# Split latent scores, projection pieces in the window attention, a first unit spread over the input's chunks, and earlier weight halves

## The chip, the core and the metric

The program runs on one core of a Trainium2 chip. Its engines are PE (TensorE, matrix products; PEld is its weight load), DVE (VectorE), ACT (ScalarE), POOL (GpSimd) and SP (SyncE, which here only issues DMAs). The metric is the time of one execution on the device in microseconds (us). All tensors are float32 in HBM.

## The reference

Two blocks run one after the other on a sequence of 512 tokens of width 1024, the first with 16 meta tokens ahead of it (528 in all).

```python
# first block
h = h + 0.5 * swiglu(rmsnorm(h, ffn1_norm), w1, w3, w2)          # d_ff 2816
q, k, v, u, g_attn, g_ssm = split(rmsnorm(h, mix_norm) @ w_in)
attn = sliding_window_attention(q, k, v, sinks)                  # 16 heads of 64, 4 key heads, blocks of 128
y = gelu(s5_ssm(u, ...))
ssm = (y @ ssm_glu_a) * sigmoid(y @ ssm_glu_b)
h = h + (sigmoid(g_attn) * attn + sigmoid(g_ssm) * ssm) @ w_out
h = h + 0.5 * swiglu(rmsnorm(h, ffn2_norm), w1, w3, w2)
x = rmsnorm(h, final_norm)[:, 16:]
# second block, layer 0: latent attention, 16 heads (128 without and 64 with rotation); layer 1: gated linear attention
c_q, c_kv, k_r = split(x @ w_in)                                 # 512, 256, 64
q = rms_norm(c_q) @ w_uq; k_nope = rms_norm(c_kv) @ w_uk; v = rms_norm(c_kv) @ w_uv
s = (q_nope . k_nope + rope(q_rope) . rope(k_r)) * scale         # per block of 128 queries, keys up to its end
m = softmax(mask(s)) @ v @ w_o
x = layer_norm(ALPHA * x + m); x = layer_norm(ALPHA * x + conv_ffn(x)); x = x + sigmoid(x @ w_gate + b) * (p @ w_proj)
```

## The kernel before

Activations lie transposed in SBUF, the width in 8 chunks of 128 partitions and the tokens along the free axis. A float32 product with weights is made as three `float32r` products: `mm3` (L565 to L568) multiplies high by high, high by low and low by high halves, with a weight load each. ACT writes the high half of a weight unit (128 output columns, 8 chunks) from the raw DMA buffer (`ahead_hi`, L539), DVE the low half (`ahead_lo`, L554); `feed_hi`/`feed_lo` mark the use of a unit and prepare so many units ahead. SP loads raw weights into three buffers; a buffer is reloaded when its last low half is made. A unit is 24 matmuls of 512 columns, or 48 of 264 columns in two halves of the tokens. Each engine runs its own list in the order in which the code is written; every wait is by a semaphore. `Banks` hands out the 8 PSUM banks in turn (`bk.take`) and makes PE wait until the engine that read a bank has freed it.

The stages that the change touches:

- **Setup** (`setup_*`). SP loads x in two halves of the width, 4 DMAs each, then two weights. ACT's queue loads all the small vectors of tile 0 (`vrows`, 9 DMAs). PE turns the vectors (L888), the meta tokens (L902) and x (L908, 32 transposes). Per chunk DVE copies to H (L933), ACT makes the gained high half (L813) and the square (L772), DVE the low half (L820), and POOL adds up the squares (L782). The first unit, "f1" 0, then runs in `ffn_pe` as `lin`: all 8 chunks of the tokens' first half, then all of the second.
- **State space scan** (`ssm_*`), 8 steps hq; weights of the window attention's first projections (`HEAD`: q0, q1, ga0, ga1) are fed at its end. After it ACT and DVE wait in `ssm_over` for the last y DMA, copy K, and feed the rest of `HEAD`.
- **Window attention** (`window_*`): 16 pairs (head group, block), pipelined over 20 steps i. In step i PE does values(i-4) (L1850, L1854), a whole projection unit in the steps of `WITH_UNIT` and at 17, the turns of the probabilities (i-3) (L1816, L1821), and scores(i) (L1756). DVE does softmax(i-1) (L1769, L1773), normalise(i-2) (L1795 to L1803), values (L1866), a weight's low half, its copies of the turned probabilities (L1839), the scaled projection (L836), and steps of the gelu of y. ACT does the exponentials (L1786), the high half and its copies of the turned probabilities (L1837).
- **Latent attention** (`latent_*`): 8 pairs of heads, 18 steps i, a pair's projections in every even step. In an even step PE makes qn0, qn1, qr, kn0, kn1 (`queries_pe`), the output of head i-3 (L2395), the values' projection, the turn of head i-2 (L2367), and the scores of head i (L2319, L2320), for which queries and keys stand in plain float32: 4 sets with 128, 256, 384 and 512 columns, two matmuls each. ACT copies QN and KN out of PSUM (L2282, L2286); DVE rotates the queries in `rope_dve` (4 copies of 32 partitions, L2174, and three operations, L2176 to L2180).
- **`lin_start`**, at the start of three units together (both up-projections of the convolution layers, and the `pg` gates): chunk k of units 0 and 1, and chunk k-1 of unit 2, behind each other.

## Time and profile before

| | us |
|---|---|
| median of 3 runs | 2745.61 |
| lowest and highest | 2744.53, 2750.54 |
| the profiled execution | 2743.8 |
| its span on the core | 2742.0 |
| PE busy in the span | 2676.6 |
| DVE busy | 1674.5 |
| ACT busy | 1015.2 |

The span is what the engines' records cover; 1.8 us lie around it. A busy time is the union of an engine's records. On PE a record lasts longer than the distance to the next one, since matmuls are pipelined, so the price of a matmul is read from the distance of two starts. The granted clock (PEclk) is the part of full speed that PE was given; it is 1.2 or 2.4 GHz at any moment, so a mean between 0.5 and 1 tells how much of a stretch was at 1.2.

### The profile page before, as it was taken

To read this page: it belongs to the slowest core of one execution; us is meant where nothing else is said; L and a number is where in the kernel's file an instruction comes from. 1 tells how busy PE (TensorE), PEld (TensorE's weight loads), DVE (VectorE), ACT (ScalarE), POOL (GpSimd) and SP (SyncE) were. 2 spreads that over 40 slices of the span, in tenths; PEclk is the share of its full clock that TensorE was granted. 3 is DMA by queue.
4 is the path that set the end of the run, shared out by engine and by line. 5 is a ranking of instruction groups with operands and counts; after the bars stand their busy time and mean duration, and the time that the engine had idled before them with its cause. 6 is when DMAs were issued, how large, how long until landed. Compare 5 with 4: busy or idle time off the path is not lost.

```text
span 2742.0 us, 35232 instructions
## 1 busy us (share of the span) xinstructions
PE 2676.6 (98%) x14595; PEld 2244.8 (82%) x14595; DVE 1674.5 (61%) x2553; ACT 1015.2 (37%) x1625; POOL 348.2 (13%) x361
## 2 busy tenths in 40 slices
PE   6999999988899999999999999999999999999999
PEld 6999999866687888887667688888887878888887
DVE  6754755668556544546664667737764467764765
ACT  3321333134334222333442435424454244542435
POOL 1133423020001000011000040000221014000031
PEclk9999999999899999999999999999999999999999
DMA  5243344421132233322111132332322212232231
GB/s 144 77 123 108 104 137 126 167 74 33 33 108 96 92 100 108 89 77 66 43 65 47 58 100 78 90 103 77 114 95 85 85 46 70 85 108 92 90 103 62
DMA packets 292727, 244.02 MB, mean 89 GB/s; under 512 B 19837, under 2 KB 285575, under 8 KB 292567
## 3 DMA queue, kind: packets, MB, share of 16 engines
q1 hardware_dynamic: 282503, 226.40, 26.1%
q0 software_dynamic: 5616, 13.22, 1.6%
q8 instruction: 115, 1.88, 0.3%
q10 hardware_dynamic: 4448, 2.16, 0.3%
q14 instruction: 45, 0.37, 0.0%
HBM read 230.70 MB, written 13.14 MB: 89 GB/s over the span
## 4 chain that ended last, share of the span: by engine, by line
PE 87%; DVE 8%; ACT 2%; issue 1%; DMA 1%; POOL 1%; ACTq 0%; SPq 0%; POOLq 0%; DVEq 0%
PE ps L566 26%; PE ps L567 25%; PE ps L568 25%; PE ps L2320 2%; PE ps L2319 2%; DVE ul L554 2%; PE ps L751 1%; PE ps L2395 1%; DVE rbuf L766 1%; PE ps L2367 1%; ACT S L1786 1%; ACT uh L539 1%; PE ps L3116 1%; PE ps L3092 1%; DVE tmp L2174 1%
## 5 line engine op out<-in xcount | busy, mean ns | idle before, releaser
L554 DVE TENSOR_TENSOR ul<-raw,uh 128x1024 fp32r<-128x1024 f32 (+3 forms) x416 | 526.5, 1289 | 340.5 <-ACT uh L539 340.1
L566 PE MATMUL ps<-OH,uh 128*128 128x512 f32 (+1 forms) x1736 | 646.6, 372 | 3.6 <-DVE ul L554 2.4
L568 PE MATMUL ps<-OH,ul 128*128 128x512 f32 (+1 forms) x1736 | 638.7, 368 | 0.0
L567 PE MATMUL ps<-OL,uh 128*128 128x512 f32 (+1 forms) x1736 | 638.5, 368 | 0.0
L539 ACT CAST uh<-raw 128x1024 fp32r<-128x1024 f32 (+3 forms) x416 | 411.9, 1025 | 158.3 <-PE ps L568 128.6
L566 PEld LDWEIGHTS ps<-OH,uh 128*128 128x128 f32 x1736 | 327.3, 189 | 66.6 <-issue 7.3
L567 PEld LDWEIGHTS ps<-OL,uh 128*128 128x128 f32 x1736 | 327.4, 189 | 55.2 <-issue 2.4
L568 PEld LDWEIGHTS ps<-OH,ul 128*128 128x128 f32 x1736 | 327.3, 189 | 54.6
L566 PE MATMUL ps<-XH,uh 128*128 128x264 f32 (+1 forms) x992 | 314.1, 317 | 13.4 <-DVE ul L554 8.1
L567 PE MATMUL ps<-HL,uh 128*128 128x512 f32 (+2 forms) x946 | 320.3, 339 | 0.0
L566 PE MATMUL ps<-HH,uh 128*128 128x512 f32 (+2 forms) x946 | 320.1, 338 | 0.0
L568 PE MATMUL ps<-HH,ul 128*128 128x512 f32 (+2 forms) x946 | 318.9, 337 | 0.0
L567 PE MATMUL ps<-XL,uh 128*128 128x264 f32 (+1 forms) x992 | 309.5, 312 | 0.0
L568 PE MATMUL ps<-XH,ul 128*128 128x264 f32 (+1 forms) x992 | 308.6, 311 | 0.0
L566 PEld LDWEIGHTS ps<-XH,uh 128*128 128x128 f32 x992 | 191.5, 193 | 31.1 <-DVE ul L554 8.8
L568 PEld LDWEIGHTS ps<-XH,ul 128*128 128x128 f32 x992 | 191.7, 193 | 9.1
L567 PEld LDWEIGHTS ps<-XL,uh 128*128 128x128 f32 x992 | 191.5, 193 | 8.5
L566 PEld LDWEIGHTS ps<-HH,uh 128*128 128x128 f32 x946 | 177.8, 188 | 22.8 <-issue 0.9
L567 PEld LDWEIGHTS ps<-HL,uh 128*128 128x128 f32 x946 | 177.7, 188 | 20.8 <-issue 0.5
L568 PEld LDWEIGHTS ps<-HH,ul 128*128 128x128 f32 x946 | 177.9, 188 | 19.7
L782 POOL TENSOR_TENSOR acc<-acc,tmp 128x512 f32<-128x512 f32 (+2 forms) x56 | 70.3, 1255 | 697.6 <-ACT tmp L772 693.1
L2552 POOL TENSOR_TENSOR acc<-H 128x512 f32<-128x512 f32 x4 | 8.6, 2149 | 974.3 <-DVE H L2791 623.2
(434 smaller groups left out, 3710.8 us busy)
## 6 DMA issues: line engine op xcount, KB each, us to landing
raw<-in_ffn_w SPq DMA_DIRECT2D x40, 1024.0 KB, 5.0
raw<-in_ffn_w_up SPq DMA_DIRECT2D x40, 1024.0 KB, 5.0
raw<-in_ffn_w SPq DMA_DIRECT2D x32, 704.0 KB, 4.3
raw<-in_ffn_w_down SPq DMA_DIRECT2D x32, 704.0 KB, 4.3
raw<-in_w_in SPq DMA_DIRECT2D x16, 1024.0 KB, 5.4
raw<-in_gla_w_in SPq DMA_DIRECT2D x12, 1024.0 KB, 5.0
raw<-in_mla_w_o SPq DMA_DIRECT2D x8, 1024.0 KB, 4.8
raw<-in_ple_w_gate SPq DMA_DIRECT2D x8, 1024.0 KB, 4.9
```

Of the source, the lines that this page charges most:

```text
L539: e.copy(h, src).then_inc(*s_whi.up((u, j)))
L554: e.tensor_tensor(l, src, h.bitcast(F32), SUB).then_inc(*s_wlo.up(("unit", u)))
L566: e.matmul(o, wh, xh, start=first, stop=False)
L567: e.matmul(o, wh, xl, start=False, stop=False)
L568: return e.matmul(o, wl, xh, start=False, stop=last)
L751: i = e.matmul(psum[:, b, 0:n], ones[:, :], tile[:, t0:t0 + n], start=j == 0, stop=j == len(parts) - 1)
L766: e.reciprocal(r[:, t0:t0 + n], r[:, t0:t0 + n]).then_inc(*s_dv.up((tag, "r", hf)))
L782: e.tensor_tensor(a, a, tmps[k - 1][:, t0:t0 + n], ADD).then_inc(*s_pool.up(*((tag, "acc", k, hf) for hf in hfs)))
L1786: e.activation(S_[:, r, 0:ntot], S_[:, r, 0:ntot], ACT.Exp, bias=z[:, 1, r:r + 1], accum_out=z[:, 3, r:r + 1]).then_inc(*s_fn.up())
L2174: e.tensor_copy(s[32 * k:32 * k + 32, :], P(key, 512, slice(32 * (k ^ 1), 32 * (k ^ 1) + 32))).then_inc(*s_dv.up())
L2319: e.matmul(psum[:, b, 0:N], QN[:, hh, 128 * n:128 * n + 128], KN[:, hh, 0:N], start=True, stop=False)
L2320: e.matmul(psum[:, b, 0:N], QR[p0:p0 + 64, 128 * n:128 * n + 128], KR[p0:p0 + 64, 0:N], start=False, stop=True).then_inc(*s_mm.up(("ms", h ...
```

## The change

Six things change together.

1. **Setup.** Only the vector `ffn1_norm` is loaded and turned ahead of x (`g1row`, `g1`); the rest of tile 0 is turned after the first sums of squares. The first weight's DMA is issued between the halves of x. PE turns x chunk by chunk; the last four chunks' turns alternate with the first unit's chunks, each for both halves of the tokens. Only unit 0's halves are made inside the chunk loop, unit 1's behind it. A dummy activation stands ahead of the loop on ACT.
2. **Scan's end.** Three weight units ahead are fed there in place of one.
3. **Window attention.** The 13 units (12 and the first "gs") run in pieces of chunks, `CHUNKS[i]` in step i: the rest of a begun unit behind values(i-4), a new unit's first chunks behind scores(i). They hold bank 3; the others take banks 0 to 2. DVE and ACT swap the order of some operations in a step.
4. **Latent scores.** Queries and keys are split into `float32r` halves: QNH, QNL, KNH, KNL; the rotated query's halves lie in the two halves of the partitions of one tile QA, the rotated key's halves in KRH and KRL (both hold the key twice). A set has five matmuls and at least 256 columns. The four copies of the rotation move from DVE to ACT.
5. **Latent weights.** The units uk, uv and the next uq are fed behind the copies of the step (`ahead_*`).
6. **`lin_start`.** Unit 2 runs two chunks behind.

```diff
@@ setup_sp, setup_act, setup_pe, setup_dve
-                    e.dma_start(xin[:, i, cs], x[i * 128:(i + 1) * 128, cs]).then_inc(*d_x[i].up(half))
+                    e.dma_start(xin[:, i, cs], x[i * 128:(i + 1) * 128, cs]).then_inc(*d_x[half].up("x"))
                 if half == 0:
                     e.dma_start(xme[:, :], A["meta_tokens"]).then_inc(*d_xme.up("x"))
+                    loads(e, 1)
...
+            d_g1.wait_ge(e, "row")
+            e.transpose(psum[:, b, 0:8], g1row[:, :], ident[0:8, 0:8]).then_inc(*s_mm.up("g1"))
+            for c in range(2):
+                turn_input_pe(e, c)
...
+            for c in range(2, 4):
+                turn_input_pe(e, c)
+            u = next_unit(e, "f1")
...
+            for k in range(8):
+                if k < 4:
+                    turn_input_pe(e, 4 + k)
+                s_lo.wait_ge(e, ("ffn1", k))
+                for (t0, n), key in zip(H1, keys):
+                    i = mm3(e, psum[:, bk.of[key], 0:n], hi[:, k, :], lo[:, k, :], XH[:, k, t0:t0 + n],
+                            XL[:, k, t0:t0 + n], k == 0, k == 7)
...
+            e.activation(misc[:, 3:4], one, ACT.Identity, scale=one).then_inc(*s_fn.up())
             for c in range(8):
                 if c == 4:
-                    feed_hi(e, "f1")
+                    feed_hi(e, "f1", 0)
...
+            ahead_hi(e, 1)
@@ lin_start
-            for k in range(9):
+            for k in range(10):
...
-                    if 0 <= k - j // 2 < 8:
-                        chunk(u, key, 0, k - j // 2)
+                    late = 2 * (j // 2)
+                    if 0 <= k - late < 8:
+                        chunk(u, key, 0, k - late)
@@ ssm_act, hq == 7, and ssm_dve, hq == 6
-                    feed_hi(e, HEAD[0][0])
+                    feed_hi(e, HEAD[0][0], 3)
...
-                    feed_lo(e, HEAD[0][0])
+                    feed_lo(e, HEAD[0][0], 3)
@@ window_pe
-        WITH_UNIT = (0, 1, 3, 4, 5, 6, 8, 9, 10, 11, 13, 15)
+        ALONG = [("q" if n < 2 else "ga", 2 * g + n % 2) for g in range(1, 4) for n in range(4)] + [("gs", 0)]
+        CHUNKS = (8, 8, 8, 7, 7, 7, 6, 6, 6, 6, 6, 6, 5, 5, 5, 3, 2, 2, 1, 0)
...
-            bk.limit(4)
+            bk.limit(3)
             for i in range(20):
                 if i >= 4:
                     values_pe(e, i - 4)
-                if q_ga(i):
-                    name, c = q_ga(i)
-                    lin(e, name, MIX, HR, (name, c))
-                if i == 17:
-                    lin(e, "gs", MIX, HR, ("gs", 0))
+                along_pe(e, i, True)
                 if 3 <= i <= 18:
                     turn_pe(e, i - 3)
                 if i < 16:
                     scores_pe(e, i)
+                along_pe(e, i, False)
@@ rope, queries, scores
+            for k in range(4):
+                e.copy(rope_tile(key)[32 * k:32 * k + 32, :], P(key, 512, slice(32 * (k ^ 1), 32 * (k ^ 1) + 32))).then_inc(
+                    *s_cp.up(("rope",) + key))
...
-            for k in range(4):
-                e.tensor_copy(s[32 * k:32 * k + 32, :], P(key, 512, slice(32 * (k ^ 1), 32 * (k ^ 1) + 32))).then_inc(
-                    *s_dv.up())
...
-                e.copy(QN[:, hh, :], P(("qn", p, hh, 0))).then_inc(*bk.free(s_cp, ("qn", p, hh, 0), ("qn", p, hh)))
+                e.copy(QNH[:, hh, :], P(("qn", p, hh, 0))).then_inc(*s_hi.up(("qn", p, hh)))
...
+        def queries_turned_act(e, p):
+            s_dv.wait_ge(e, ("rope", "qr", p, 0))
+            for hh in range(2):
+                rows = slice(64 * hh, 64 * hh + 64)
+                e.copy(QA[rows, hh, :], QR[rows, :]).then_inc(*s_hi.up(("qr", p, hh)))
+            feed_hi(e, "uk", 0)
...
+                e.tensor_tensor(QNL[hh][:, :], P(("qn", p, hh, 0)), QNH[:, hh, :].bitcast(F32), SUB).then_inc(
...
+                e.tensor_tensor(KNL[:, hh, :], P(("kn", p, hh, 0)), KNH[:, hh, :].bitcast(F32), SUB).then_inc(
...
+                e.tensor_tensor(QA[other, hh, :], QR[rows, :], QA[rows, hh, :].bitcast(F32), SUB).then_inc(
...
-                N = 128 * (n + 1)
+                N = max(128 * (n + 1), 256)
                 b = bk.take(e, ("ms", h, n), 4 + n)
-                e.matmul(psum[:, b, 0:N], QN[:, hh, 128 * n:128 * n + 128], KN[:, hh, 0:N], start=True, stop=False)
-                e.matmul(psum[:, b, 0:N], QR[p0:p0 + 64, 128 * n:128 * n + 128], KR[p0:p0 + 64, 0:N], start=False,
-                         stop=True).then_inc(*s_mm.up(("ms", h, n), ("ms", h)))
+                o, q = psum[:, b, 0:N], slice(128 * n, 128 * n + 128)
+                mm3(e, o, QNH[:, hh, q], QNL[hh][:, q], KNH[:, hh, 0:N], KNL[:, hh, 0:N], True, False)
+                e.matmul(o, QA[:, hh, q], KRH[:, 0:N], start=False, stop=False)
+                e.matmul(o, QA[:, hh, q], KRL[:, 0:N], start=False, stop=True).then_inc(
+                    *s_mm.up(("ms", h, n), ("ms", h)))
```

PE's list at the start of the program, before: `ident` is the identity, `xin` the input as loaded, `uh`/`ul` the weight's halves.

```order
L888 MATMUL ps<-ident,vrows 128x112
L902 MATMUL ps<-ident,xme 128x16 x8
L908 MATMUL ps<-ident,xin 128x128 x32
L566 MATMUL ps<-XH,uh 128x264
L567 MATMUL ps<-XL,uh 128x264
L568 MATMUL ps<-XH,ul 128x264
```

After:

```order
L934 MATMUL ps<-ident,g1row 128x8
L925 MATMUL ps<-ident,xin 128x128 x8
L940 MATMUL ps<-ident,xme 128x16 x8
L925 MATMUL ps<-ident,xin 128x128 x12
L572 MATMUL ps<-XH,uh 128x264
L573 MATMUL ps<-XL,uh 128x264
L574 MATMUL ps<-XH,ul 128x264
L572 MATMUL ps<-XH,uh 128x264
L573 MATMUL ps<-XL,uh 128x264
L574 MATMUL ps<-XH,ul 128x264
L925 MATMUL ps<-ident,xin 128x128 x4
```

The first unit's chunks now stand between the turns of x; chunk 0 has both halves of the tokens (two triples) before the next turn.

PE's list in the window attention from the last scores of step 7 (K and KS are keys, Q queries, PT turned probabilities, VB and V values), before:

```order
L1756 MATMUL ps<-KS,Q 128x256
L1756 MATMUL ps<-K,Q 128x16
L1756 MATMUL ps<-K,Q 128x256
L1850 MATMUL ps<-PT,VB 128x256
L1854 MATMUL ps<-PT,V 64x256 x2
L566 MATMUL ps<-XH,uh 128x512
L567 MATMUL ps<-XL,uh 128x512
```

After:

```order
L1830 MATMUL ps<-K,Q 128x16
L1830 MATMUL ps<-K,Q 128x256
L572 MATMUL ps<-XH,uh 128x512
L573 MATMUL ps<-XL,uh 128x512
L574 MATMUL ps<-XH,ul 128x512
L1924 MATMUL ps<-PT,VB 128x256
L1928 MATMUL ps<-PT,V 64x256 x2
L572 MATMUL ps<-XH,uh 128x512
```

Between the scores and the next values stood nothing; now a chunk of a projection unit does (seven, six, five and three of them in steps 3 to 6).

PE's list in the latent attention, one head's scores, before:

```order
L2319 MATMUL ps<-KN,QN 128x128
L2320 MATMUL ps<-KR,QR 128x128
L2319 MATMUL ps<-KN,QN 128x256
L2320 MATMUL ps<-KR,QR 128x256
L2319 MATMUL ps<-KN,QN 128x384
L2320 MATMUL ps<-KR,QR 128x384
L2319 MATMUL ps<-KN,QN 128x512
L2320 MATMUL ps<-KR,QR 128x512
```

After, its second and third set:

```order
L572 MATMUL ps<-KNH,QNH 128x256
L573 MATMUL ps<-KNL,QNH 128x256
L574 MATMUL ps<-KNH,QNL_158 128x256
L2432 MATMUL ps<-KRH,QA 128x256
L2433 MATMUL ps<-KRL,QA 128x256
L572 MATMUL ps<-KNH,QNH 128x384
L573 MATMUL ps<-KNL,QNH 128x384
L574 MATMUL ps<-KNH,QNL_158 128x384
L2432 MATMUL ps<-KRH,QA 128x384
L2433 MATMUL ps<-KRL,QA 128x384
```

A set of two float32 matmuls has become one of five `float32r` matmuls; the first set of the head, 128 columns before, has 256 now.

## Rows read from the trace of the kernel before

**Rows 1.** The page: busy us, share of the span and instructions by engine.

```profile
PE 2676.6 (98%) x14595; PEld 2244.8 (82%) x14595; DVE 1674.5 (61%) x2553; ACT 1015.2 (37%) x1625; POOL 348.2 (13%) x361
```

**Rows 2.** Stretches: us, busy us (x instructions), granted clock, DMA share, GB/s.

```profile
0.00:39.24 39.24, 20.08 (x98) 18.31 (x99) 19.13 (x23) 14.36 (x21) 11.54 (x19) 0.83 0.72 197
31.60:37.40 5.80, 5.78 (x27) 5.78 (x28) 1.10 (x1) 0.00 (x0) 0.00 (x0) 0.52 0.62 192
565.50:734.20 168.70, 145.95 (x794) 105.80 (x792) 120.43 (x245) 67.92 (x203) 8.33 (x16) 0.92 0.12 35
1285.50:1600.00 314.50, 310.67 (x1344) 215.52 (x1344) 189.74 (x360) 121.31 (x279) 2.15 (x1) 0.99 0.16 54
1362.90:1395.70 32.80, 32.38 (x142) 21.64 (x141) 21.65 (x43) 14.02 (x35) 0.00 (x0) 1.00 0.12 41
```

**Rows 3.** PE in order of time, setup: start, us, line, [idle before, releaser].

```profile
10.24 0.42 PE L888 MATMUL ps<-ident,vrows 112*128 112x112 f32 x1 [10.24 <-DMA vrows<-in_ple_b_gate]
...
39.24 0.49 PE L888 MATMUL ps<-ident,vrows 118*128 118x118 f32 x3
...
44.20 0.39 PE L566 MATMUL ps<-XH,uh 128*128 128x264 f32 x1 [1.58 <-DVE tmp L836]
```

**Rows 4.** DVE in order of time, setup.

```profile
12.71 0.69 DVE L933 COPY H<-ps 128x512 f32<-128x512 f32 x1 [0.60 <-PE ps L908]
...
15.55 0.77 DVE L820 SCALAR_TENSOR_TENSOR XL<-H,cv,XH 128x528 fp32r<-128x528 f32 x1 [1.29 <-ACT XH L813]
...
21.58 3.97 DVE L554 TENSOR_TENSOR ul<-raw,uh 128x1024 fp32r<-128x1024 f32 x2
...
29.08 2.49 DVE L820 SCALAR_TENSOR_TENSOR XL<-H,cv,XH 128x528 fp32r<-128x528 f32 x2
```

**Rows 5.** SP's issues at the start; issues from 1.7 to 2.6, median to landing.

```profile
0.73 1.86 SPq L846 DMA_DIRECT2D xin<-in_x  x4
...
xin<-in_x SPq DMA_DIRECT2D x2, 256.0 KB, 4.5
```

**Rows 6.** PE in order of time, scan's end and window attention.

```profile
552.94 0.80 PE L566 MATMUL ps<-XH,uh 128*128 128x512 f32 x1 [2.47 <-DVE ul L554]
...
659.83 0.70 PE L1850 MATMUL ps<-PT,VB 64*128 64x256 f32 x2
...
676.58 1.19 PE L1850 MATMUL ps<-PT,VB 64*128 64x256 f32 x2 [4.04 <-ACT PT L1837]
```

**Rows 7.** PE in order of time, one latent head's scores, to its end.

```profile
1324.45 0.39 PE L2319 MATMUL ps<-KN,QN 128*128 128x128 f32 x2
...
1328.12 1.12 PE L2319 MATMUL ps<-KN,QN 128*128 128x512 f32 x2
...
1330.22 0.50 PE L566 MATMUL ps<-CQH,uh 128*128 128x512 f32 x1
```

**Rows 8.** PE, float32r matmuls of 512 and of 256 columns, neighbours.

```profile
1330.56 0.39 PE L567 MATMUL ps<-CQL,uh 128*128 128x512 f32 x1
1330.79 0.40 PE L568 MATMUL ps<-CQH,ul 128*128 128x512 f32 x1
...
1376.23 0.28 PE L567 MATMUL ps<-ul,CKH 128*128 128x256 f32 x1
1376.35 0.28 PE L568 MATMUL ps<-uh,CKL 128*128 128x256 f32 x1
```

**Rows 9.** DVE in latent step 6; PE at the scores of steps 2 and 6.

```profile
1371.43 2.84 DVE L2174 COPY tmp<-ps 32x512 f32<-32x512 f32 x4 [4.22 <-PE ps L568]
...
1378.10 0.68 DVE L2409 TENSOR_TENSOR OL<-ps,OH 128x512 fp32r<-128x512 f32 x1
...
1315.25 0.46 PE L2319 MATMUL ps<-KN,QN 128*128 128x128 f32 x2 [0.67 <-DVE QR L2180]
...
1380.75 0.39 PE L2319 MATMUL ps<-KN,QN 128*128 128x128 f32 x2
```

**Rows 10.** PE inside `lin_start` of layer 0, the sums' wait.

```profile
1633.61 0.70 PE L751 MATMUL ps<-H,ones 128*128 128x256 f32 x2 [0.29 <-DVE H L2454]
```

More of the change, by code:

```diff
@@ L286, in program @@
         d_raw = [landing(f"d_raw{i}") for i in range(NRAW)]
-        d_x, d_xme = [landing(f"d_x{i}") for i in range(4)], landing("d_xme")
+        d_x, d_xme, d_g1 = [landing(f"d_x{i}") for i in range(2)], landing("d_xme"), landing("d_g1")
         d_vr = [landing(f"d_vr{i}") for i in range(4)]
@@ L459, in program @@
         r0 = 0
[L460 to L461 removed]
+        for name, ap in (("mix", A["mix_norm"][0]), ("ffn2", A["ffn2_norm"][0]), ("final", A["final_norm"])):
             r0 = rows(name, r8(ap), 0, r0, 8)
@@ L587, in lin, with lin_piece @@
             return u
+        def lin_piece(e, name, X, t0, n, key, bank, k0, k1):
+            xh, xl, tag = X
+            if k0 == 0:
+                piece_of[key] = next_unit(e, name)
+                bk.take(e, key, bank)
+            u = piece_of[key]
+            hi, lo, _ = halves_of(u)
+            for k in range(k0, k1):
+                s_lo.wait_ge(e, (tag, k))
+                i = mm3(e, psum[:, bk.of[key], 0:n], hi[:, k, :], lo[:, k, :], xh[:, k, t0:t0 + n],
+                        xl[:, k, t0:t0 + n], k == 0, k == 7)
+            if k1 == 8:
+                i.then_inc(*s_mm.up(key, ("unit", u)))
+        piece_of = {}
         def lin_pair(e, names, X, halves, keys):
@@ L903, in setup_pe @@
             t.then_inc(*s_mm.up("xm"))
-            for c in range(8):
-                b = bk.take(e, ("xt", c))
-                for i in range(4):
-                    d_x[i].wait_ge(e, c // 4)
-                    t = e.transpose(psum[:, b, i * 128:(i + 1) * 128], xin[:, i, c * 128:(c + 1) * 128], ident[:, :])
-                t.then_inc(*s_mm.up(("xt", c)))
+            for c in range(2, 4):
+                turn_input_pe(e, c)
+            u = next_unit(e, "f1")
+            keys = [("F1", "a", 0, hf) for hf in range(2)]
+            for key in keys:
+                bk.take(e, key)
+            hi, lo, _ = halves_of(u)
+            for k in range(8):
[5 more added lines that the diff above has]
+                            XL[:, k, t0:t0 + n], k == 0, k == 7)
+                    if k == 7:
+                        i.then_inc(*s_mm.up(key, *([("unit", u)] if key == keys[1] else [])))
         def setup_act(e):
+            e.dma_start(g1row[:, :], r8(A["ffn1_norm"][0])).then_inc(*d_g1.up("row"))
             for r, n, ap in vparts[0]:
                 e.dma_start(vrows[r:r + n, 0, :], ap).then_inc(*d_vr[0].up("rows"))
-            s_dv.wait_ge(e, ("col", 0))
+            s_cst.wait_ge(e, "ones")
+            e.activation(misc[:, 3:4], one, ACT.Identity, scale=one).then_inc(*s_fn.up())
+            s_dv.wait_ge(e, "g1")
             for c in range(8):
                 if c == 4:
-                    feed_hi(e, "f1")
+                    feed_hi(e, "f1", 0)
                 s_dv.wait_ge(e, ("h0", c))
@@ L933, in setup_dve, with ffn_pe @@
                     e.tensor_copy(H[:, c, 16:528], P(("xt", c))).then_inc(*bk.free(s_dv, ("xt", c), ("h0", c)))
-                if c == 5:
-                    feed_lo(e, "f1")
                 if c:
                     gained_dve(e, "ffn1", X1, c - 1, H[:, c - 1, :], "ffn1")
-        def ffn_pe(e, st, names, X, halves, side, param, ends, before=None, norm=None, shift=None, late=2):
+            ahead_lo(e, 1)
+        def ffn_pe(e, st, names, X, halves, side, param, ends, before=None, norm=None, fed=0, shift=None, late=2):
             n1, n3, n2 = names
@@ L1407, in norm @@
                 rms_pe(e, "ffn1", H1)
-                for tile in range(1, 4):
+                bk.limit(8, 0)
+                for tile in range(4):
                     columns_pe(e, tile)
-            ffn_pe(e, "F1", F1, X1, H1, side, param, 8, starts(param, side, lambda: param_pe(e), lambda: s5_pe(e)), norm)
+            ffn_pe(e, "F1", F1, X1, H1, side, param, 8, starts(param, side, lambda: param_pe(e), lambda: s5_pe(e)), norm, 1)
         def first_act(e):
@@ L2492, in latent_act @@
                     latent_output_act(e, i - 3)
+                if i % 2 == 0 and i < 16:
+                    queries_turned_act(e, i // 2)
                 if i == 0:
```

164 lines of the change are left out of this document (110 added, 54 removed).

## The prediction

> **What bounds the kernel now.** I read the page first: PE is busy for 2676.6 of 2742.0 us, so almost everything that is not PE's work or PE's clock is hidden [rows 1]. A gain has to come from three places only: PE's idle time, stretches in which PE works at 1.2 instead of 2.4 GHz, and PE's own work. The table of stretches shows where they lie [rows 2]. Up to 39.24 PE is busy for 20.08 us. In the window attention (565.5 to 734.2) PE is idle for 168.70 - 145.95 = 22.75 us and has a mean granted clock of 0.92. In the latent attention (1285.5 to 1600) it is busy for 310.67 of 314.50 at 0.99: nothing is to be had from waits there, only from PE's work. Those are the three places that the change touches. The sum is made against the profiled execution (2743.8, of which 2742.0 is the span), 1.8 below the median 2745.6; I carry the difference over.
>
> **Setup.** Before, PE starts at 10.24, released by the last of the nine small vectors; DVE starts its chunk loop at 12.71 [rows 3, 4]. x's first half is issued from 0.73 to about 1.7 + 0.9 = 2.6 and lands 4.5 after issue, so by about 6.6 [rows 5]. With only `ffn1_norm` ahead of it, PE starts there. Ahead of DVE's loop then lie two chunks' turns and the meta tokens, in all about 2.7 (the distance from PE's start to DVE's loop is 12.71 - 10.24 = 2.5 now). DVE's loop starts at 9.3, 3.4 earlier. The loop now lasts until 29.08 + 2.49 = 31.57, so 18.9. It loses ACT's table load (a wait of 1.29) and one of two low halves (half of 3.97, about 2.0), and keeps the rest, 15.6; it would end at 24.9 [rows 4]. Behind it PE now runs until 37.4, for 5.8 us, at clock 0.52: the second half of the tokens at half speed, until 39.24 the sums [rows 2, 3]. After, both halves of a chunk follow it, and at the end only the last chunk's six matmuls remain (1.3 at the low clock). Sums: 1.8, to 3 at the low clock. That ends at about 28 to 29.5, 10 to 11 earlier. The wait of 1.58 at 44.20 for a bank of unit 0 goes, since the banks are handed out differently, but the first bank after the sums now waits for ACT's root (0.5 to 1), and the warm-up of the clock, which was over at 37.4, now falls into the next unit: 1 to 2.7 given back. Net **10**, bounds 6 and 13. All of it is ahead of PE's solid stretch, so it stays, unless the parameters of the scan arrive late; their DMAs are issued before 31.6 in any case.
>
> **Scan's end.** At 552.94 PE waits 2.47 for a low half [rows 6], which ACT and DVE begin only after their wait for the last y DMA. Feeding it before that wait costs both engines nothing there, since PE is in matrix products of the scan and of q0 meanwhile. **2.5**, bounds 0 and 2.5.
>
> **Window attention.** PE's work is the same 13 units, values, turns and scores. What can go is 22.75 of idle time and the low clock. Clock 0.92 with two levels means 16% of 168.7, 27 us, at 1.2 GHz. Idle time is part of it, so matmuls lose between (27 - 22.75) / 2 = 2 and 27 / 2 = 13.5; the values' first two matmuls take 1.19 behind the wait of 4.04, and 0.70 elsewhere [rows 2, 6], so the waits are followed by low clock, and I take 10. The floor for PE is then 168.7 - 33 = 136. Before, values(i-4) stood right behind scores(i-1) and waited there for copies that DVE makes late in its step; now up to 8 chunks of a unit (0.23 x 3 = 0.7 each [rows 8]) cover that. The next bound is DVE: 120.43 busy [rows 2], and in steps 6, 7, 10 and 11 it still waits over 1 us for ACT's high half, about 5 in all. 126 against 136 is close, the two engines hand work back and forth twice in a step, and a new unit's first chunks can only start when DVE has finished its step. I leave a third of the loss in place: **22**, bounds 8 and 31.
>
> **Latent scores.** One head's scores take 1330.22 - 1324.45 = 5.77; its largest set 1330.22 - 1328.12 = 2.10, so 1.05 per float32 matmul of 512 columns [rows 7]. A `float32r` matmul of 512 columns takes 0.23, one of 256 columns 0.12, with its own weight load each time [rows 8]; 384 lies between, 0.175. After: 5 x (0.12 + 0.12 + 0.175 + 0.23) = 3.2. Saved 2.55 per head, 16 heads, 40.8. What hides the new work: a pair takes 32.8 now and would take 27.7. DVE is busy for 21.65 of it, ACT for 14.02 [rows 2]. DVE loses 4 copies (2.84) and gains 4 differences and 2 of half the partitions, at 0.68 each, 4.1 [rows 9]: 22.9. ACT gains 6 copies at 0.6 to 0.7: 18. Both fit. The chain from qr to the scores is longer: 4 copies 2.84, three operations 2.07, two copies to QA 1.2, two differences 1.36, with the keys' two (1.36) partly between: 7.5 to 8.8. In step 6 qr was ready at 1371.4 and the scores began at 1380.75: 9.3 of cover [rows 9]. That is enough by 0.5 to 1.8. In step 2 there is neither output nor values; PE waited 0.67 already, and now 2 to 4 more. Ahead of step 0 DVE has the key's low half to make, 0.5 to 1. **38**, bounds 27 (a wait of 1.5 in each pair) and 42.
>
> Here a rule speaks for less. The row shows 1.05 against 0.23, a ratio of 4.6 [rows 7, 8]. The Trainium skill, in "FP8 and Floating Point Precision", section "TensorE Precision Notes", says that true FP32 is 4 passes through the PE array. By it a head would take 4.6 before, 1.4 more than after, and the saving would be 22 instead of 41. I go by the row, which is this very instruction.
>
> **`lin_start`.** All three units' weights are waited for ahead of the first chunk, so a later unit 2 meets no later weight. In layer 0 and 1 its first chunk stood ahead of the sums, which wait 0.29 for H [rows 10]; without it that wait grows by 3 x 0.12. Two places: **-0.6**, bounds -1.5 and 0.5. The latent weights' new place costs nothing: PE waited for no latent weight in steps 0 to 17, and ACT and DVE have 15 and 5 us free in a pair.
>
> Sum: 10 + 2.5 + 22 + 38 - 0.6 = 72. 2743.8 - 72 = 2671.8; carried to the median **2674**.
>
> **Rivals.** (a) *The window attention gains little.* The wait for DVE's copies turns into a wait for DVE's low half at the end of its step, or for bank 3 which all pieces share. For it: DVE is busy for 120 of 169 us already, and for 120 of 147 if the term comes true [rows 2]. Against it: 22.75 of idle time that DVE did not need. Gain 5 in place of 22: 2691. (b) *The latent chain is late in every pair.* If the chain takes 10.5 in place of 8.8, PE waits 1 to 3 in 8 pairs: the latent term is 20, 2692. (c) *Both*, or (a) with a setup of 5: 2705. (d) *Slower.* In the latent attention a wait in front of each pair's scores that is long enough to bring PE to 1.2 GHz, as behind the 4.04 in the window [rows 6], doubles what follows. A pair saves 5.1; the other terms bring 34. It decides from 5.1 + 34 / 8 = 9.4 lost per pair, say 6 of wait and 4 at the low clock: 2750 or more. For it: the chain crosses four times between ACT and DVE. Against it: the cover of 9.3 is as long as the chain. (e) *The split scores don't do what they say*: a `float32r` matmul whose weights are activations costs what a float32 one does. Rows with 256 columns, where activations are the weights, show 0.12 [rows 8]; 5 matmuls in place of 2 would give over 2800.
>
> **How the numbers follow.** The forecast has 0.66, from 2660 to 2688. (a) 0.12 and (b) 0.09, both 2688 to 2700; (c) 0.05, to 2715; better than 2660 0.05, both soft terms at their ends; (d) 0.02; (e) 0.01. The range leaves out (c), (d), (e) and half of the better ones: 2656 to 2700. A measurement can tell 0.2% (5.5 us) from no change. Slower by that is (d) and (e), 0.03; within it 0.01; faster 0.96.
>
> **What would show it.** In the profile after: PE's first record near 6.6, the first sums ending before 30; no wait at the first "ga"; the window attention from its first unit to its last values in 140 to 155 us, with a clock of at least 0.96; a latent head's scores in 3.2 and a pair in 27.5 to 28.5; PE's busy time down by about 50. I am wrong if a latent pair takes over 30, or the window stage over 160.

## The result and the profile after

The changed kernel takes **2698.66 us** (median of 4 runs, 2696.21 to 2702.24) against 2745.07 for the kernel before on the same chip (median of 4), a ratio of 0.983 with a 95% interval of 0.981 to 0.985. The profiled execution is the one of 2696.21, its span is 2694.4. The direction and the range held (the range by 1.3 us), the forecast of 2674 did not: 46 us by medians and 48 by the two profiled executions came in place of 72. The question of this part is where the other 24 went.

First, how much earlier PE reaches the same line of the program. The lead is the start before minus the start after.

| PE reaches | before | after | lead |
|---|---|---|---|
| end of the setup's sums | 39.24 | 30.99 | 8.3 |
| last turn of the scan's parameters | 341.7 | 332.9 | 8.8 |
| start of the window's head groups | 565.5 | 548.5 | 17.0 |
| first unit behind the last values | 734.2 | 702.7 | 31.5 |
| the latent query norm (32 one-column matmuls) | 1282.1 | 1249.6 | 32.5 |
| first sum of layer 0 | 1598.4 | 1550.1 | 48.3 |
| end | 2742.0 | 2694.4 | 47.6 |

Setup gave 9, scan and scan's end 8, the window attention 14.5, the latent attention 16. The last two were down for 22 and 38.

Second, what each stage consists of. The stretches of the kernel after, as in [rows 2] (us, busy us of PE, PEld, DVE, ACT, POOL, granted clock, DMA share, GB/s):

```profile
0.00:30.99 30.99, 17.06 (x97) 15.71 (x98) 16.79 (x21) 14.87 (x22) 10.52 (x19) 1.00 0.78 212
548.50:702.70 154.20, 140.77 (x794) 99.91 (x793) 120.76 (x245) 67.60 (x203) 9.18 (x18) 0.99 0.13 39
1249.60:1550.10 300.50, 281.46 (x1434) 234.28 (x1433) 199.70 (x379) 145.73 (x327) 2.15 (x1) 0.96 0.17 56
1353.74:1382.52 28.78, 27.24 (x148) 22.66 (x149) 22.49 (x46) 16.89 (x40) 0.00 (x0) 1.00 0.25 84
```

The trace's clock records begin at 23.2, and what lies ahead of them counts as 1.00; so the 1.00 of the first row says nothing of the time up to 23.2 (see Setup below). The same latent stretch before, from the query norm to layer 0:

```profile
1282.10:1598.40 316.30, 312.47 (x1370) 217.94 (x1369) 191.78 (x362) 121.90 (x280) 2.15 (x1) 0.99 0.16 53
```

I split each stretch into idle time, time lost to 1.2 GHz (over slices of 2 us: PE's busy time x (1 - granted clock)), and the rest, which is PE's work at full clock. A wait shorter than the overlap of two records (a record of 0.39 where the next start follows after 0.23) doesn't show as idle time and counts as work. Seven kernels with the same instructions in the latent stretch have 270.4 to 271.3 of it, two others with the same list on PE (both below) 268.9 and 267.1.

| | length | idle | lost to the clock | work |
|---|---|---|---|---|
| window before | 168.7 | 22.8 | 11.3 | 134.6 |
| window after | 154.2 | 13.4 | 1.4 | 139.4 |
| latent before | 316.3 | 3.8 | 1.7 | 310.8 |
| latent after | 300.5 | 19.0 | 11.0 | 270.5 |

So in the latent attention PE's work fell by 40.3, just as forecast (40.8), and 15.2 of new waits and 9.3 of low clock took 24.5 of it back. In the window attention the loss fell by 19.3, nearly the 22 of the forecast, and PE's work rose by 4.8, for which the sum had no term. The 1.4 of low clock is a good draw: with the same list of PE in the window, ten other profiles of the experiments below lost 1.4 to 6.2 from the first scores to the first unit behind the last values (the changed kernel's 1.5 there), so the stage's gain is 10 to 14.5.

What PE waited for in the latent stretch of the kernel after (the view of waits: us in total, times, longest; OH and OL are the high and low half of a head's output, KNL and QNL the low halves of keys and queries, PTm the turned probabilities):

```profile
PE ps L572 <- DVE OL L2522: 9.5, 6, 3.0
PE ps L572 <- DVE ul L560: 2.8, 1, 2.8
PE ps L2508 <- DVE PTm L2500: 1.8, 1, 1.8
PE ps L572 <- DVE QA L2407: 1.6, 1, 1.6
PE ps L2480 <- DVE KNL L2400: 1.4, 1, 1.4
PE ps L572 <- DVE SS L2448: 1.0, 1, 1.0
```

The first row is the wait that repeats. Its place, engine by engine in order of time (PE; DVE; ACT):

```profile
1345.29 2.32 PE L2508 MATMUL ps<-PTm,VT 128*128 128x512 f32 x8
...
1353.74 0.47 PE L572 MATMUL ps<-CQH,uh 128*128 128x512 f32 x1 [1.43 <-DVE OL L2522]
...
1343.80 2.43 DVE L560 TENSOR_TENSOR ul<-raw,uh 128x1024 fp32r<-128x1024 f32 x3 [1.09 <-ACT uh L545]
...
1350.86 0.69 DVE L2451 TENSOR_REDUCE zst<-SS 128x1 f32<-128x512 f32 x1
1352.90 0.69 DVE L2522 TENSOR_TENSOR OL<-ps,OH 128x512 fp32r<-128x512 f32 x1 [1.35 <-ACT OH L2518]
...
1351.58 0.72 ACT L2458 ACTIVATE SS<-SS,zst 128x512 f32<-128x512 f32 x1 [0.67 <-DVE zst L2451]
1352.30 0.56 ACT L2518 CAST OH<-ps 128x512 fp32r<-128x512 f32 x1
```

A pair's first unit needs the bank that holds the last output. DVE frees it with OL, and OL waits for ACT's OH, which stands in ACT's queue behind four exponentials, although PE had finished that output's matmuls (the first row) at 1347.6, some 5 us before. And DVE comes to this step late: at 1343.80 it makes three low halves of later weights, ahead of its normalisation and masks.

### The profile page after: what moved, and what is told of

It is laid out like the page before. It is cut to its first block, busy times and chain, and to the rows that moved or that the text cites. A ratio compares the mean times of both kernels' runs of the same rounds, so it can differ in the third digit from the quotient of the medians.

```text
span 2694.4 us, 35439 instructions
## 1 busy us (share of the span) xinstructions
PE 2631.1 (98%) x14660; PEld 2247.5 (83%) x14660; DVE 1677.5 (62%) x2567; ACT 1042.2 (39%) x1679; POOL 346.5 (13%) x361
## 3 DMA queue, kind: packets, MB, share of 16 engines
q1 hardware_dynamic: 282503, 226.40, 26.7%
## 4 chain that ended last, share of the span: by engine, by line
PE 88%; DVE 7%; ACT 3%; issue 1%; DMA 1%; POOL 0%; SPq 0%; ACTq 0%; POOLq 0%; DVEq 0%
PE ps L572 27%; PE ps L573 26%; PE ps L574 26%; DVE ul L560 1%; PE ps L775 1%; ACT uh L545 1%; PE ps L2508 1%; PE ps L1590 1%; DVE zst L2451 1%; DVE SS L2448 1%; PE ps L3239 1%; PE ps L3215 1%; DVE rbuf L790 0%; ACT S L1860 0%; PE ps L2480 0%
## 5 line engine op out<-in xcount | busy, mean ns | idle before, releaser
L572 PEld LDWEIGHTS ps<-HH,uh 128*128 128x128 f32 x946 | 177.7, 188 | 22.8 <-issue 0.9
```

What stands on the lines that cost most here:

```text
L572: e.matmul(o, wh, xh, start=first, stop=False)
```

## The experiments

Each kernel differs from the changed one by what its diff shows; each was timed against the kernel before on its own chip. That kernel's median was 2741.9 to 2745.1 there, so a difference of 3 us between two rows of the table is not one of the kernels by itself.

| kernel | median us | ratio to before, 95% |
|---|---|---|
| latent attention as before | 2720.9 | 0.992 (0.990 to 0.994) |
| window order as before | 2712.8 | 0.988 (0.986 to 0.990) |
| setup as before | 2711.3 | 0.989 (0.987 to 0.990) |
| one weight at the scan's end | 2701.8 | 0.985 (0.984 to 0.987) |
| window units uncut | 2705.0 | 0.987 (0.985 to 0.990) |
| third unit one chunk behind | 2697.5 (one run) | |
| the changed kernel again | 2699.7 | 0.984 (0.982 to 0.986) |
| OH first | 2686.3 | 0.980 (0.978 to 0.982) |
| OH first, projection's weight earlier | 2689.5 | 0.981 (0.979 to 0.983) |
| the same, normalisation later | 2689.2 | 0.981 (0.979 to 0.982) |
| latent weights at their old places | 2686.7 | 0.980 (0.977 to 0.982) |
| old places, and both queues reordered | 2678.8 | 0.977 (0.975 to 0.978) |

**Each part undone.** Four kernels, each with one part of the change taken back.

*The latent attention as before.*

> The changed kernel with the latent attention of the kernel before (float32 scores, weights fed ahead of the copies); all else changed. Theory A (the split scores save PE 5.1 us per pair, 41 in all, but 15 us of new waits for DVE and 10 us at the low clock take 25 back, so the part is worth what the landmarks show, 15.4): 2698.7 + 15.4 = 2714, 2711 to 2717. Theory B (the prediction's term of 38 is right and 23 us are lost elsewhere because of it, outside this stage): 2735 or more. In the trace under A: the 32 one-column matmuls and what follows lie at 1.00 but for some 5 us, no wait of over 1 us ahead of a pair, sum of PE's waits in the stage about 3 us.

2720.9, outside both. The stage itself says A: its latent stretch takes 317.9 (before 316.3, after 300.5), with 3.8 idle. The other 5 us have their place between the scan and the merge (below: from the last turn of the scan's parameters to the small turn of the positions behind the merge, 332.9 to 855.8 in the changed kernel). The two kernels share that code and wait equally long in it (15.4 and 15.6), but this profile (the slowest execution of its four) lost 17.9 us to the clock there and that of the changed kernel (the fastest of its four) 6.4. More on that below.

*The window attention's order as before.*

> The changed kernel with the window attention's order of before (a whole unit behind the values, turn copies behind the softmax); all else changed. Theory A (the part is worth its stage alone, 168.7 - 154.2 = 14.6): 2713, 2711 to 2716. Theory B (part of the low clock that went before the stage, at 529 to 541, hangs on it, or the stage's gain is in part the earlier parts'): 2718 or more, or below 2709. The waits of 4 us for DVE's copies ahead of the values return; their sum in the stage is about 20 us, and the mean clock of the stage falls from 0.97 to about 0.92.

2712.8 (A); the idle time between scan and merge is 24.4 in place of 15.6. Its profiled execution took 2703.5 and the other three 2712.4 to 2713.5; why is told under the clock.

*The setup as before.*

> The changed kernel with the setup of before (all nine vectors and x's four row blocks ahead of PE, the first unit in two passes behind the chunks). Theory A (all 8.8 us of the setup's lead are kept to the end): 2707.5, 2706 to 2709. Theory B (the scan's tables or the parameters' transfers are late by the same time either way, so that a part of the lead is lost before the scan ends): less than 2704. Theory C (the half clock at 529 to 541 hangs on when the scan starts): 2712 or more.

At the last turn of the scan's parameters this kernel is 9.6 us behind the changed one and at the window's first scores 10.0: the setup's lead is kept to there. The total, 2711.3, lies between A's and C's ranges. Its profile lost 12.7 to the clock between scan and merge where the changed kernel's lost 6.4, but none of it at the place that C names.

*One weight ahead at the scan's end.*

```
-                    feed_hi(e, HEAD[0][0], 3)
+                    feed_hi(e, HEAD[0][0])
```

> The changed kernel with one weight in place of three made ahead at the scan's end. Before, PE waited 2.47 us there and worked at half clock from 529 to 541; after, neither. Theory A (the clock of that stretch belongs to the wait ahead of it or around it): the low clock comes back with the wait, 2698.7 + 2.5 + 5.4 = 2706.5, 2704 to 2708. Theory B (the stretch's clock belongs to something else, such as the shift of 8.8 us or a state of the chip): only the wait of 2.5 comes back, 2701, 2699 to 2703. The first row of the matmuls from 529 tells them apart: 13 us against 8 for the same work.

The wait is back:

```profile
544.69 0.50 PE L572 MATMUL ps<-XH,uh 128*128 128x512 f32 x1 [2.51 <-DVE ul L560]
```

and the time, 2701.8, is B's. But low clock is back too, at 522 to 529, ahead of the wait, which is neither theory. The kernels that kept the three weights settle it.

**The clock where nothing changed.**

> The changed kernel again, unaltered, on the same chip as the runs beside it. Theory A (the low clock between 455 and 545 and behind the short waits of the window attention comes and goes with the alignment of equal work, as the runs so far show in that stretch: 6 us lost in the changed kernel's profile, 8 to 18 in five others with the same instructions there): 2696 to 2705, the stretch from the scan's start to the end of the merge 523 to 533 us and the idle time of PE in it within 0.5 of 15.6. Theory B (the half clock at 529 to 541 went with the change): none between 515 and 545.

2699.7; between scan and merge 15.8 idle and 4.5 lost to the clock, none of it between 515 and 545 (B so far), and with 521.6 the stretch is shorter than A had it. But the kernel with OH first (below), whose instructions up to the latent attention are the same, fell to half clock from 523 to 533. The same part of the scan in the kernel before (where it lies 9 us later), in this one and in that one:

```profile
530.00:538.00 8.00, 8.00 (x31) 7.23 (x31) 4.99 (x10) 2.32 (x5) 0.54 (x1) 0.50 0.26 92
...
522.00:530.00 8.00, 8.00 (x49) 6.96 (x47) 6.13 (x9) 3.17 (x4) 0.54 (x1) 1.00 0.45 141
...
522.00:530.00 8.00, 8.00 (x39) 7.41 (x39) 5.59 (x14) 2.85 (x6) 0.54 (x1) 0.55 0.46 167
```

Of the twelve profiles with the three weights five fell to half clock there and seven did not. So the 5 us that the kernel before lost at 529 to 539 and the changed kernel's profile did not are chance, and A holds. The latent stretch shows it best, since seven of the profiles have the very same instructions and 19.0 us of idle time in it. Six take 299.4 to 300.7 and lose 9.5 to 11.2; the seventh, with the window's old order, takes 293.3 and loses 2.9, and it is the execution of 2703.5 that came out 9 us ahead of its fellows (its row, to be read against that of the changed kernel above, 1249.60 to 1550.10):

```profile
1264.20:1557.50 293.30, 274.26 (x1434) 227.73 (x1433) 199.49 (x379) 145.59 (x327) 2.15 (x1) 0.99 0.18 57
```

At one place, the wait of 2.79 in step 10, the two show it side by side. First the changed kernel, the wait ending at 1401.50, then the other, the wait ending at 1410.52:

```profile
1401.00:1403.00 2.00, 1.50 (x5) 1.22 (x6) 1.58 (x2) 2.00 (x4) 0.00 (x0) 0.81 0.00 0
1403.00:1405.00 2.00, 2.00 (x6) 1.52 (x6) 0.00 (x0) 0.98 (x2) 0.00 (x0) 0.50 0.54 173
...
1410.00:1414.00 4.00, 3.48 (x15) 2.90 (x16) 1.61 (x2) 3.01 (x4) 0.00 (x0) 1.00 0.26 85
1414.00:1418.00 4.00, 4.00 (x19) 3.30 (x19) 1.70 (x2) 1.06 (x1) 0.00 (x0) 1.00 0.54 181
```

Whether the clock falls to 1.2 GHz behind a short wait depends on more than the wait. The Trainium skill, in "TensorE: Matmul & The Clock Gate", section "The HAM clock gate", says that the chip judges activity on a beat that runs free of the kernel, so that the warm-up of one and the same kernel comes out differently by where its first matmul lands. The rows would agree with that for drops in the middle of a kernel too; no run here tests it directly.

**The wait for the outputs' bank.**

```
             for i in range(19):
+                first = i >= 3 and (i % 2 == 1 or i == 16)
+                if first:
+                    latent_output_act(e, i - 3)
                 if 1 <= i <= 16:
                     latent_softmax_act(e, i - 1)
...
-                if i >= 3:
+                if i >= 3 and not first:
                     latent_output_act(e, i - 3)
```

> The changed kernel with one move on ACT: in the latent attention's odd steps and in step 16 the copy OH of head i-3 stands ahead of the four exponentials of head i-1, not behind them. Theory A (PE's 1.43 us ahead of a pair is the wait for the bank of the output, which DVE frees with OL, which waits 1.35 for OH behind the exponentials): the four waits of 1.43 and 1.3 to 1.5 of the 3.05 at the end go, a pair takes 27.4 in place of 28.8, and some of the low clock behind the 3.05: 2698.7 - 7 to - 11, so 2688 to 2692. Rival (DVE's own work is the bound of a pair, or the next wait, for QA ahead of the scores, takes the place): a pair stays at 28.5 or more and the time within 2 us of 2698.7.

2686.3, A by its mechanism and 2 us better than its range. A pair takes 27.3. PE's waits for OL fell from 9.5 to 2.3 and the one for PTm from 1.8 to 0.3; the latent stretch went from 300.5 to 287.9, with 8.5 us less of idle time and 4.5 less of low clock. By medians of whole runs the gain is 12.3 us.

```
+                if i == 9:
+                    ahead_hi(e, 4)
```

(and the same for the low halves on DVE)

> The kernel of the previous run with the first output-projection unit's halves made at the end of step 9 instead of step 10. Theory (the wait of 2.79 for its low half in step 10 comes from two halves being made one after the other behind the values' copies, and the step of low clock behind it costs another 2): 4 to 5 us less than the previous run. Rival (the later start of DVE's normalisation and masks in step 10 gives it back, or the weight's place in the ring is still in use, so that ACT waits there): no gain, or up to 2 slower.

The wait of 2.8 did go, but waits of 1.00 for QNL and 0.43 for KNL came in the same step: the idle time fell by 1.2, the stretch by 1.1. In the total nothing can be told (2689.5, 3 us slower, where one kernel's executions differ by as much). The rival was nearer.

**The place of the later weights.** The prediction gave it no cost, and the rows at 1343.80 speak against that.

```
             rope_act(e, ("qr", p, 0))
+            feed_hi(e, "uk", 1 if p == 1 else 2)
...
         def queries_turned_act(e, p):
-            feed_hi(e, "uk", 0)
...
-                if i % 2 == 0 and i < 16 and i != 10:
-                    ahead_hi(e, 1 if i == 2 else 2)
```

(the same on DVE; the values' weights feed the next one again)

> The changed kernel with the latent attention's later weights made where the kernel before makes them (the pair's later weights ahead of the keys' copies, the next pair's at its own start), the split scores kept. Theory A (with 9.3 us of cover and a chain of 7.5 to 8.8 the place of the weights decides: 2 to 3 us of weight halves on ACT and DVE inside the chain make PE wait ahead of each pair's scores): 8 to 20 us slower than the changed kernel, 2707 to 2719, waits for QA in each pair. Theory B (as the prediction had it, ACT and DVE have room and the place of the weights costs and gives nothing): within 3 us of 2698.7.

**Both theories fell: it is 12 to 13 us faster**, 2686.7 (2699.7 for the changed kernel on the same chip), with the split scores kept. The waits in its latent stretch:

```profile
PE ps L572 <- DVE KNL L2401: 6.7, 6, 1.4
PE ps L572 <- DVE OL L2522: 3.0, 2, 2.3
PE ps L572 <- DVE QA L2408: 1.6, 1, 1.6
PE ps L2480 <- DVE KNL L2401: 1.4, 1, 1.4
...
1339.40 0.39 PE L572 MATMUL ps<-uh,CKH 128*128 128x256 f32 x1 [1.40 <-DVE KNL L2401]
```

The weights' halves now stand inside the chain, and it is indeed late, by 1.40 at the values' unit in most pairs (the last row, out of PE's timeline), but nothing more: the only wait for QA is that of step 2, which the changed kernel has too. In exchange DVE reaches the odd step's normalisation earlier, the wait of 1.43 for OL, those of 2.8 for the projection's low half and of 1.8 for PTm are gone, and with them all low clock but that behind the one-column matmuls: idle 13.0, clock 3.4, the stretch 285.4. The move was meant to free the copies, and it put a block of 3.5 us (the 2.43 of low halves and 1.09 of wait for the high ones) in front of the softmax of each odd step, where DVE was the engine that was behind.

The last kernel takes the waits of both. The weights stay at the old places; ACT, which idles for 3.1 to 3.4 us ahead of its exponentials, makes the pair's two high halves there, DVE makes both low halves right behind its masks, and OH goes first in odd steps.

```
+                first = i >= 3 and (i % 2 == 1 or i == 16)
+                if first:
+                    latent_output_act(e, i - 3)
+                if i % 2 == 0 and i < 16:
+                    feed_hi(e, "uq", 2 if i == 2 else 3)
                 if 1 <= i <= 16:
                     latent_softmax_act(e, i - 1)
...
-            feed_lo(e, "uq", 2)
+            feed_lo(e, "uq", 2 if p == 1 else 3)
```

> The kernel with the latent weights at their old places (the run that came out 12 us below the changed kernel), and three moves on top: OH ahead of the exponentials in odd steps and in step 16; ACT makes a pair's key and value weights' high halves before the exponentials of the even step, where it idles for 3.1 to 3.4 us; DVE makes both low halves right behind its softmax, where it now waits 1.4 for the first high half, and none between rope and the keys' differences. Theory A (ACT's and DVE's serial chain from the exponentials to the keys' low halves holds the bank for which PE waits 1.40 in each pair): that wait falls to under 0.4, pairs from 28.3 to 27.0 to 27.4, PE's idle time in the latent attention from 13.0 to 4 to 7, the kernel 2677 to 2683. Rival (the wait moves on to the scores, for QA, or to the outputs' bank): pairs stay at 28 or more and the time at 2684 to 2690.

2678.8, ratio 0.977 (0.975 to 0.978): A, and faster than both kernels of this case. It makes three moves at once, and no run tells what each is worth. A pair takes 26.7. Of the waits these are left, in step 2 (the first two) and in the last two steps:

```profile
PE ps L572 <- DVE QA L2407: 1.6, 1, 1.6
PE ps L2479 <- DVE KNL L2400: 1.4, 1, 1.4
PE ps L572 <- DVE OL L2521: 1.1, 2, 0.7
PE ps L2479 <- ACT VT L2418: 0.6, 1, 0.6
PE ps L2507 <- ACT PTm L2497: 0.3, 1, 0.3
```

The stretch takes 278.4 with 5.1 idle and 6.1 of low clock. Its units follow the scores at 1325.49 with no wait. With the prediction's saving this stretch should have taken 316.3 - 38 = 278.3. That the two agree to 0.1 is luck, since the sum had no low clock in it.

**The window attention.**

```
-        CHUNKS = (8, 8, 8, 7, 7, 7, 6, 6, 6, 6, 6, 6, 5, 5, 5, 3, 2, 2, 1, 0)
+        CHUNKS = tuple(8 if i in (0, 1, 2, 4, 5, 6, 8, 9, 10, 11, 12, 13, 16) else 0 for i in range(20))
```

> The changed kernel with the 13 units of the window attention uncut: eight chunks behind the scores of steps 0, 1, 2, 4, 5, 6, 8 to 13 and 16, none in the others, the rest of the order as in the changed kernel. What it tells: PE's work in the stage at full clock came out 4.7 us above before (140.8 - 1.4 against 146.0 - 11.3), which the prediction had at nothing. Theory A (each cut costs PE: one chunk alone takes 0.81 us against 0.71 in a whole unit, and a change between two kinds of work 0.1 to 0.2): busy at full clock falls by 2 to 4 us. Rival (the 4.7 is an error of reading, from records at low clock): it stays within 1. For the time: pieces cover the wait ahead of the values, whole units don't; waits of 2 to 4 us in front of the values and in steps 3, 7, 14, 15 come back and the stage takes 158 to 166 in place of 154 to 157, the kernel 2702 to 2710.

The time is as expected (2705.0). The work is not: length less idle time less clock loss, between scan and merge, is 499.8 to 501.4 in eleven profiles with the new order and pieces, 500.0 here without pieces, and 496.3 and 496.1 in the two with the old order. So the order costs PE 4 to 5 us of work, and the cuts of the units about 1 of it, less than theory A's 2 to 4. The distances between starts (idle time taken out, counted at full clock) say where more than half lies. Of a projection's matmuls of 512 columns, the first behind another kind of work is followed by the next after 0.31 us, the last by the other work after 0.27 (0.32 where that is the values), and one in the middle after 0.23. The new order has 36 such beginnings and ends, the old 21, this kernel 22; together the projections' matmuls take 92.97 us in the changed kernel, 90.13 with the old order and 91.18 here. The other 2 us lie in the values', scores' and turns' matmuls. Whether a change of kind costs PE this or a short wait hides in it is open. In the latent attention it is at least in part a wait: from the last matmul of a head's scores to the next unit PE takes 0.32 in the changed kernel and 0.23 in the two kernels with the weights at their old places, whose list on PE is the same.

```
+                late = any(k1 - k0 == 3 and k1 == 8 for _, k0, k1 in pieces_of(i, True))
-                if 2 <= i <= 17:
+                if 2 <= i <= 17 and not late:
                     normalise_dve(e, i - 2)
...
+                if 2 <= i <= 17 and late:
+                    normalise_dve(e, i - 2)
```

(the second one behind the scaled projections)

> The kernel with OH ahead of the exponentials and the first projection unit's halves in step 9, and in the window attention DVE's normalisation of head group i-2 behind the scaled projection, in the steps that end a unit with three chunks. Theory A (bank 3, which all pieces share, comes free late because DVE normalises first): the two waits of 2.4 us for Q fall to under 1 us each, with the low clock behind them 2 to 6 less than that kernel: 2682 to 2687. Rival (DVE is late as a whole, so another wait takes their place): the idle time of PE in the stage stays at 13 to 16 and the time at 2686 to 2690.

The rival: the two waits stayed, 4.7 in all, and so did the time (2689.2). One of them is 2.42 in the changed kernel (first row) and 2.41 here (PE, then DVE and ACT in order of time):

```profile
605.15 0.47 PE L572 MATMUL ps<-XH,uh 128*128 128x512 f32 x1 [2.42 <-DVE Q L860]
...
611.51 0.77 PE L572 MATMUL ps<-XH,uh 128*128 128x512 f32 x1 [2.41 <-DVE sst L1869]
...
606.29 0.48 DVE L1940 SCALAR_TENSOR_TENSOR Mg<-Mg,ps 128x128 f32<-128x128 f32 x2
609.54 1.23 DVE L560 TENSOR_TENSOR ul<-raw,uh 128x1024 fp32r<-128x1024 f32 x1 [2.77 <-ACT uh L545]
610.68 0.68 DVE L860 TENSOR_TENSOR Q<-ps,mbuf 128x512 f32<-128x512 f32 x1
...
608.38 0.19 ACT L1863 ACTIVATE sst<-sst 128x4 f32<-128x4 f32 x1
608.48 1.03 ACT L545 CAST uh<-raw 128x1024 fp32r<-128x1024 f32 x1
```

DVE isn't busy there but waits 2.77 for ACT's high half, which ACT makes behind its exponentials; the scaled projection that frees the bank stands behind the low half and ends at 611.36. (The row names the small operation on `sst` behind it in the same queue.) The move only took work out of the gap: DVE waited 1.62 for the high half there in the changed kernel. Making the high half ahead of the exponentials was not tried here; in the latent attention that move worked.

**The third joint unit.**

```
-                    late = 2 * (j // 2)
-                    if 0 <= k - late < 8:
-                        chunk(u, key, 0, k - late)
+                    if 0 <= k - j // 2 < 8:
+                        chunk(u, key, 0, k - j // 2)
```

> The changed kernel with the third joint unit one chunk behind in place of two. Theory A (the later start costs 0.3 at each of the two places where sums or a late chunk are waited for, nothing is gained): the stretch from the first layer's start to the second layer's end is shorter by 0.3 to 0.7. Theory B (it avoids a wait for a weight somewhere): longer by 0.3 or more. The landmarks tell it to 0.1, the total time does not.

A. The sums of the two layers wait twice 0.61 in the changed kernel, twice 0.3 here and before:

```profile
1585.33 0.70 PE L775 MATMUL ps<-H,ones 128*128 128x256 f32 x2 [0.61 <-DVE H L2567]
```

No wait for a weight differs between the two.

## Point by point

**What bounds the kernel** held: PE is busy for 2631.1 of 2694.4 us, 45.5 less than before (about 50 forecast).

**Setup, forecast 10: 9.** The first transposes of x started at 7.35, not 6.6, and DVE's loop at 10.53, not 9.3; it ended at 28.3, not 24.9, and the sums at 30.99, not ahead of 30. The term that was mis-sized is the loop, 17.8 long and not 15.6. PE, ACT and DVE now take turns at chunk 4:

```profile
18.31 1.12 PE L925 MATMUL ps<-ident,xin 128*128 128x128 f32 x4 [6.12 <-DVE ul L560]
...
17.03 1.23 DVE L560 TENSOR_TENSOR ul<-raw,uh 128x1024 fp32r<-128x1024 f32 x1 [1.17 <-ACT uh L545]
19.46 0.69 DVE L985 COPY H<-ps 128x512 f32<-128x512 f32 x1 [1.21 <-PE ps L925]
```

and PE's transposes of the later chunks stand behind matmuls that need the low half, which the sum had not looked for. Part of that was made up by a charge that never came, and part of it is that charge in another place. The first unit's matmuls of 264 columns followed each other by 0.22 up to 22.7, as they did before at a granted clock of 0.52, and by 0.12 from 23.3 on:

```profile
20.10 0.42 PE L573 MATMUL ps<-XL,uh 128*128 128x264 f32 x1
20.32 0.42 PE L574 MATMUL ps<-XH,ul 128*128 128x264 f32 x1
...
23.78 0.28 PE L572 MATMUL ps<-XH,uh 128*128 128x264 f32 x1
23.90 0.29 PE L573 MATMUL ps<-XL,uh 128*128 128x264 f32 x1
```

So the low clock fell into the loop, where DVE waited 1.21 and 0.81 for PE's turns; the 12 slow matmuls cost some 1.2 us there (an estimate, 12 times the difference of 0.10). The 1 to 2.7 us for it behind the sums did not fall due. This is read from the trace; no kernel takes back one of the two alone.

**Scan's end, forecast 2.5: 2.5** of wait, as the kernel with one weight shows. The 5 us beside it were the clock's chance.

**Window, forecast 22: 14.5.** The stage took 154.2 at a clock of 0.99, inside the forecast's 140 to 155 and over its 0.96. Of the loss of 34 (22.8 idle, 11.3 clock) 14.8 stayed, where the sum left 11: more idle time than thought, 13.4, and less clock, 1.4. The step that failed is "PE's work is the same": the new order costs it 4 to 5 us, short waits that the records hide included. Rival (a) had the right places (bank 3, a low half that is late), with 5 us of waits and not 17.

**Latent, forecast 38: 16.** The price of the split scores held: a head's scores take 3.3 (forecast 3.2) and the work fell by 40.3. So the rows had the size. The rule of the Trainium skill ("FP8 and Floating Point Precision", section "TensorE Precision Notes") that true FP32 takes four passes, which gave 22, had not. Two steps failed. "The latent weights' new place costs nothing" is wrong by 12 to 13 us: it looked at free time per pair (there are 6 us of DVE and 12 of ACT, as the row of the pair shows) and not at where in DVE's queue the weights came to stand. And the cover was compared for one chain only, qr to scores, which held (the only wait for QA is the 1.6 in step 2); the one that broke is another, from the scores over DVE's masks, ACT's exponentials and OH to the bank that the next pair needs. The pair took 28.8, just over the forecast's 27.5 to 28.5 and well under the 30 that would have refuted it: rival (b)'s size by another way. Its 11 us of low clock had no term; the forecast of a 0.96 clock was made for the window alone.

**`lin_start`, forecast -0.6: -0.6**, by the two waits; its one run (2697.5) can't show it in the time.

The range of 2656 to 2700 held both medians of the changed kernel, by 1.3 and 0.3 us. That is less than its executions differ (2695.2 to 2702.9, three of the eight above 2700), so it was luck. The time lies in the part of the range that the prediction gave to (a) and (b), with 0.21, and not in the forecast's own, with 0.66. Cases (a) and (b) came true in part together, and their sum of 2705, which the range left out, was closer than the forecast.

## What to carry to other kernels

Spare time per step says that work fits, not that it costs nothing: for each block that is moved, name the instruction behind it in its queue and the bank or buffer which that frees. When PE gets faster, look again at every chain that was hidden, and first at copies that free a bank and stand behind a softmax; put them ahead of it, and put work that waits for nothing where an engine idles before a softmax. A gain in low clock in one profile is worth believing only when another kernel with the same instructions there shows it too.

## What the hardware showed that was not expected

- The same instructions with the same 19.0 us of waits lost 2.9 us to 1.2 GHz in one profile and 9.5 to 11.2 in six others. Between scan and merge, where eleven profiles have the same list on PE and 14.4 to 17.5 idle, the loss ranged from 4.5 to 17.9. Executions of one kernel differ here by 3 to 11 us, which is of that size.
- PE can be busy all the time and still fall to 1.2 GHz: in the changed kernel from 1252.0 to 1258.9, within and behind the 32 one-column matmuls (1249.6 to 1253.8), with PE busy throughout 1240 to 1260. Twelve of the 14 profiles show 6.8 us of it there, which costs 3.4; the kernel before shows 3.4 us, the one with the window's old order none.
- Moving the same window work into another order raised PE's time at full clock, short waits included, by 4 to 5 us in some 500, and by 4 with the units uncut.
- The profile's clock records can begin late (at 23.2 in the changed kernel); up to there the granted clock reads 1.00 while matmuls keep the distance of half clock, 0.22 for 0.12.
